# Token-major k, v and vs of the prompt: 32x32 block transposes and 128-byte transfers in the place of TensorE transposes

## The reference

```python
h = rms_norm(x, g_pre);  z = h @ w_in            # 1024 x 3072
q, k, v, ga, u, vs, gg = split(z)                # 512, 256, 256, 512, 512, 512, 512 columns
att  = attend(q, k, v)                           # block-sparse attention, prompt: own and past blocks of 256
u    = gelu(u);  v_rows = group_layer_norm(gelu(vs), g_sgu)      # 8 groups of 64 channels
gm   = u * (tril(w_s[g]) v_rows + b[g])          # inside chunks of 128 tokens
y    = x + rms_norm(concat(att * silu(ga), gm * silu(gg)) @ w_out, g_post)
return y, k, v, v_rows                           # k, v rows are outputs, v_rows for the sample alone
```

## Time and profile before

| | us |
|---|---|
| median of 3 runs | 288.61 |
| lowest, highest | 286.06, 288.98 |
| the profiled execution | 285.58 |
| its span, first to last instruction | 283.9 |

### The profile page before, as it was taken

The page is one execution under the profiler, slowest core; times in us unless marked ns, Lnnn a source line. Parts: engine busy times, 40 slices in busy tenths (PEclk is TensorE's granted clock), DMA queues, the critical chain, the costliest instruction groups (busy, mean ns, idle before and its releaser), DMA issues.

```text
span 283.9 us, 6071 instructions
## 1 busy us (share of the span) xinstructions
PE 272.5 (96%) x2140; PEld 237.2 (84%) x2140; DVE 196.0 (69%) x447; ACT 154.6 (54%) x353; POOL 69.7 (25%) x85
## 2 busy tenths in 40 slices
PE   8999999999999999999899999999899999999992
PEld 2789998998997887999687999998799976767881
DVE  1794886599935335826649889899979894927763
ACT  5974459541694323178886466555364563628611
POOL 4547003300311040333033452432450510000000
PEclk9999999999999999999999999999999999999998
DMA  7969993349998898831445018022007604040042
GB/s 244 330 179 223 286 244 90 135 153 274 245 315 247 260 300 216 267 112 41 149 135 172 2 37 224 1 67 84 0 2 271 193 1 148 2 149 2 18 187 109
DMA packets 37602, 43.39 MB, mean 153 GB/s; under 512 B 2963, under 2 KB 32659, under 8 KB 37572
## 3 DMA queue, kind: packets, MB, share of 16 engines
q1 hardware_dynamic: 36626, 40.25, 46.9%
q0 software_dynamic: 944, 2.75, 3.7%
q10 hardware_dynamic: 2, 0.00, 0.0%
HBM read 39.59 MB, written 3.41 MB: 151 GB/s over the span
## 4 chain that ended last, share of the span: by engine, by line
PE 75%; DVE 12%; ACT 8%; issue 3%; DVEq 0%; POOL 0%; ACTq 0%; POOLq 0%
PE Z L1386 12%; PE Z L1387 12%; PE Z L1388 12%; PE T L1307 4%; PE S L1425 3%; DVE probs L1205 3%; PE O L1524 2%; PE Z L1343 2%; PE O L1460 2%; PE S L1343 2%; PE Z L1345 2%; PE S L1344 2%; PE Z L1344 2%; PE S L1345 2%; DVE pT_lo L1211 2%
## 5 line engine op out<-in xcount | busy, mean ns | idle before, releaser
L1386 PE MATMUL Z<-act_hi,w_hi 128*128 128x256 f32 (+1 forms) x352 | 102.9, 292 | 0.6 <-ACT zvs L839 0.3
L1387 PE MATMUL Z<-act_lo,w_hi 128*128 128x256 f32 (+1 forms) x352 | 101.8, 289 | 0.0
L1388 PE MATMUL Z<-act_hi,w_lo 128*128 128x256 f32 (+1 forms) x352 | 101.5, 288 | 0.0
L1386 PEld LDWEIGHTS Z<-act_hi,w_hi 128*128 128x128 f32 x352 | 66.5, 189 | 2.9 <-issue 2.0
L1387 PEld LDWEIGHTS Z<-act_lo,w_hi 128*128 128x128 f32 x352 | 66.4, 189 | 0.0
L1388 PEld LDWEIGHTS Z<-act_hi,w_lo 128*128 128x128 f32 x352 | 66.3, 188 | 0.0
L678 POOL TENSOR_TENSOR w_lo<-w_raw,w_hi 128x1024 fp32r<-128x1024 f32 x16 | 38.2, 2389 | 67.0 <-ACT w_hi L764 67.0
L764 ACT ACTIVATE w_hi<-w_raw 128x1024 fp32r<-128x1024 f32 x32 | 33.5, 1051 | 15.0 <-DMA w_raw<-in_w_out 9.8
L980 DVE TENSOR_TENSOR w_lo<-w_raw,w_hi 128x1024 fp32r<-128x1024 f32 x16 | 19.3, 1211 | 16.0 <-ACT w_hi L764 16.0
L906 ACT ACTIVATE probs<-S,nmax 128x128 f32<-128x128 f32 (+3 forms) x32 | 16.6, 523 | 23.0 <-DVE nmax L1195 21.7
L1082 DVE STREAM_TRANSPOSE kT<-k_ring 128x1024 f32<-128x1024 f32 x16 | 19.7, 1238 | 0.6 <-PE S L1425 0.5
(11 more groups left out here) (253 smaller groups left out, 532.3 us busy)
## 6 DMA issues: line engine op xcount, KB each, us to landing
w_raw<-in_w_in SPq DMA_DIRECT2D x11, 1024.0 KB, 7.0
k_ring<-in_cache_k SPq DMA_DIRECT2D x64, 128.0 KB, 3.2
v_ring<-in_cache_v SPq DMA_DIRECT2D x64, 128.0 KB, 4.3
w_raw<-in_w_out SPq DMA_DIRECT2D x8, 512.0 KB, 4.3
x_sb<-in_x_prompt SPq DMA_DIRECT2D x4, 512.0 KB, 5.6
x_res<-in_x_prompt SPq DMA_DIRECT2D x4, 512.0 KB, 5.3
out<-y_sb SPq DMA_DIRECT2D x8, 256.0 KB, 2.0
w_raw<-in_w_in SPq DMA_DIRECT2D x2, 512.0 KB, 6.4
```

The lines of the kernel that those rows point to most:

```text
L1386: mm(out, wh[:, k, :], act_hi[:, k, cols], start=(k == 0), stop=False)
L1387: mm(out, wh[:, k, :], act_lo[:, k, cols], start=False, stop=False)
L1388: last = mm(out, wl[:, k, :], act_hi[:, k, cols], start=False, stop=(k == KD - 1))
```

## The change

For the four full token tiles the transposes on PE go. DVE turns each 128x512 tile of `kv32` (`KVB` 0 to 3: k0, k1, v0, v1) and of `zvs` (`VSB` 0 to 3) in place as 32x32 blocks. Each block then stands in the right orientation but in the wrong place, and transfers that POOL issues put it right: four for each tile, each of 32 partitions with 16 pieces of 128 bytes, 512 pieces. For k and v they go straight to the outputs; v is then read back as rows (`v_tok`, 512 KB), and one ACT and one DVE instruction of 128x1024 make `v_st` (`VST`). For vs they go to a DRAM tensor `vs_rows`, from which one transfer of 1 MB fills `vn`. The layer norm of those tiles (`VLN`) runs from `vn` in SBUF, tiles 0 and 1 behind halves 28 and 29 (behind round two's `DEX 1`), tiles 2 and 3 behind 31 and 32. `VSN 4` moves from half 31 to 24, `LN` from 32 to 33, `LNM` from 33, 35, 37, 39, 41 to 34, 36, 37, 39, 40.

New waits: POOL waits for the v transfers to land before the read back (in `KVB 3`, half 16), and for the vs transfers before the read of `vn` (in `VSB 3`, half 24); ACT waits at half 20 for `v_back`, DVE there for ACT; DVE waits at half 28 for `vs_moved`.

```diff
-    after(16, ("KVN", 4), ("KVN", 0))
-    for n, h in enumerate((17, 20, 22)):
-        after(h, ("KVN", 1 + n))
+    for j in range(4):
+        after(10 + 2 * j, ("KVB", j))
+    after(16, ("KVN", 4))
+    after(20, ("VST",))
...
-    for n, h in enumerate((24, 25, 28, 29)):
-        after(h, ("VSN", n))
+    for j in range(4):
+        after(18 + 2 * j, ("VSB", j))
+    after(24, ("VSN", 4))
+    for n, h in enumerate((28, 29)):
+        after(h, ("VLN", n))
...
-    after(31, ("VSN", 4))
-    after(32, ("LN",))
-    for n, tt in enumerate((4, 0, 1, 2, 3)):
-        after(33 + 2 * n, ("LNM", tt))
+    after(31, ("VLN", 2))
+    after(32, ("VLN", 3))
+    after(33, ("LN",))
+    for h, tt in zip((34, 36, 37, 39, 40), (4, 0, 1, 2, 3)):
+        after(h, ("LNM", tt))
... POOL
-                    pool.wait_ge(vst_done, 4)
-                    pool.wait_ge(stored_kv[1], 2 * 32)
+                    pool.wait_ge(vst_done, 1)
                     pool.dma_start(g_sgu_bc[:, :], ...)
+                elif kind == "KVB":
+                    j = s[1]
+                    out, landed = (k_prompt, stored_k) if j < 2 else (v_prompt, stored_v)
+                    rows = out[0, 0].rearrange("(b j) h d -> j b (h d)", j=32)
+                    pool.wait_ge(kv_turned, j + 1)
+                    for a in range(4):
+                        at = P * (j % 2) + 32 * a
+                        pool.dma_start(rows[:, :, at:at + 32], kv32[32 * a:32 * a + 32, j, 0:SEQ].rearrange("p (b i) -> p b i", i=32))\
+                            .then_inc(landed, 16)
+                    if j == 3:
+                        pool.wait_ge(stored_v, 8 * 16)
+                        pool.dma_start(v_tok[:, :, :], v_prompt[0, 0].rearrange("(t p) h d -> p t (h d)", p=P)).then_inc(v_back, 16)
+                elif kind == "VSB":
+                    j = s[1]
+                    rows = vs_rows.rearrange("(b j) c -> j b c", j=32)
+                    pool.wait_ge(vs_turned, j + 1)
+                    for a in range(4):
+                        at = P * j + 32 * a
+                        pool.dma_start(rows[:, :, at:at + 32], zvs[32 * a:32 * a + 32, j, 0:SEQ].rearrange("p (b i) -> p b i", i=32))\
+                            .then_inc(vs_out, 16)
+                    if j == 3:
+                        pool.wait_ge(kt_done, 16)
+                        pool.wait_ge(vs_out, 16 * 16)
+                        pool.dma_start(vn[:, 0:4, :], vs_rows.rearrange("(t p) c -> p t c", p=P)).then_inc(vs_moved, 16)
... ACT
+                elif kind == "VST":
+                    act.wait_ge(v_back, 16)
+                    nc.scalar.activation(v_st[:, :, :, 0:HD], v_tok[:, :, :].rearrange("p t (h d) -> p t h d", h=KVH), ACT.Copy).then_inc(vst_hi, 1)
+                elif kind == "VLN":
+                    act.wait_ge(centred, tt + 1)
+                    act.wait_ge(ssq_done, tt + 1)
+                    nc.scalar.activation(ln_sq[:, :], vn[:, tt, :], ACT.Square).then_inc(sq_done, 1)
... DVE
+                elif kind == "KVB":
+                    if j < 2:
+                        dve.wait_ge(k_first, 2 * j + 2)
+                    else:
+                        dve.wait_ge(z_free["act"], freed(Z_FREED_BY, HALF_AT[TILE_OF["v", j - 2], 1])[1])
+                    nc.vector.transpose(kv32[:, j, 0:SEQ], kv32[:, j, 0:SEQ]).then_inc(kv_turned, 1)
+                elif kind == "VST":
+                    dve.wait_ge(vst_hi, 1)
+                    nc.vector.tensor_tensor(v_st[:, :, :, HD:], v_tok..., v_st[:, :, :, 0:HD].bitcast(fp32), ALU.subtract).then_inc(vst_done, 1)
+                elif kind == "VSB":
+                    dve.wait_ge(z_free["act"], freed(Z_FREED_BY, HALF_AT[TILE_OF["vs", j], 1])[1])
+                    nc.vector.transpose(zvs[:, j, 0:SEQ], zvs[:, j, 0:SEQ]).then_inc(vs_turned, 1)
+                elif kind == "VLN":
+                    if tt == 0:
+                        dve.wait_ge(vs_moved, 16)
+                    link(nc.vector.tensor_reduce(ln_mu[:, 0, :], vt, AX.X, ALU.add))
+                    nc.vector.scalar_tensor_tensor(vt, ln_mu[:, 0, :]..., -1.0 / GCH, vt, ALU.mult, ALU.add).then_inc(centred, 1)
+                    dve.wait_ge(sq_done, tt + 2)
+                    nc.vector.tensor_reduce(ln_var[:, tt, :], ln_sq[:, :]..., AX.X, ALU.add).then_inc(ssq_done, 1)
```

More of the change, by code:

```diff
@@ L237, in build @@
     w_out_v = w_out[0].rearrange("(k p) c -> p k c", p=P)
+    vs_rows = nc.dram_tensor("vs_rows", [SEQ, 512], fp32).ap()
     def kv_rows(prompt, sample, tt):
@@ L291, in build @@
         R_V = region(4096 + 8192 + 10240)
-        kvn = place("kvn", [P, 2, 512], fp32, R_V)
+        v_tok = place("v_tok", [P, 4, KVW], fp32, R_V)
         ln_sq = place("ln_sq", [P, 512], fp32, R_V)
@@ L402, in build @@
         v_in = [sem(f"v_in{n}") for n in range(4)]
-        stored_kv = [sem("stored_kv0"), sem("stored_kv1")]
+        stored_k, stored_v, v_back = sem("stored_k"), sem("stored_v"), sem("v_back")
+        kv_turned, vs_turned, vs_out, vs_moved = (sem(n) for n in ("kv_turned", "vs_turned", "vs_out", "vs_moved"))
         stored_kvs = sem("stored_kvs")
@@ L636, in _ @@
             sp.wait_ge(stored_sgu, 16)
-            for n in range(2):
-                sp.wait_ge(stored_kv[n], 2 * 32)
+            sp.wait_ge(stored_k, 8 * 16)
+            sp.wait_ge(stored_v, 8 * 16)
             sp.wait_ge(stored_kvs, 32)
@@ L855, in _ @@
                     R = ROWS[tt]
-                    if 2 <= tt < 4:
-                        act.wait_ge(stored_kv[tt % 2], 32)
-                        act.wait_ge(vst_done, tt - 1)
-                    take(n, (kvn[:, tt % 2, :] if tt < 4 else kv_s[:, 0:512]), T[n % 2][0:R, :])
-                    if tt < 4:
-                        act.wait_ge(t_free["act"], freed(T_FREED_BY, n)[1])
-                        nc.scalar.activation(v_st[:, tt, :, 0:HD], kvn[:, tt % 2, KVW:].rearrange("p (h d) -> p h d", h=KVH), ACT.Copy)\
-                            .then_inc(vst_hi, 1)
+                    take(n, kv_s[:, 0:512], T[n % 2][0:R, :])
+                elif kind == "VST":
+                    act.wait_ge(v_back, 16)
+                    nc.scalar.activation(v_st[:, :, :, 0:HD], v_tok[:, :, :].rearrange("p t (h d) -> p t h d", h=KVH), ACT.Copy).then_inc(vst_hi, 1)
                 elif kind == "DEX":
@@ L1050, in _ @@
                             dve.wait_ge(t_full, T_OF["VSN", 4] + 1)
+                            dve.wait_ge(vs_moved, 16)
                         if what == "gg" and j == 0 and half == 0:
-                            dve.wait_ge(t_full, T_OF["KVN", 3] + 1)
+                            dve.wait_ge(t_full, T_OF["KVN", 4] + 1)
+                            dve.wait_ge(stored_k, 8 * 16)
+                            dve.wait_ge(stored_v, 8 * 16)
                         nc.vector.scalar_tensor_tensor(dst[:, j, cols], th[:, g % 2, 0:wide], 1.0, bank[:, 0:wide], ALU.add, ALU.mult)\
@@ L1070, in _ @@
                         .then_inc(t_free["dve"], 1)
[L1071 to L1076 removed]
+                elif kind == "KVB":
+                    j = s[1]
+                    if j < 2:
[5 more added lines that the diff above has]
+                    dve.wait_ge(vst_hi, 1)
+                    nc.vector.tensor_tensor(v_st[:, :, :, HD:], v_tok[:, :, :].rearrange("p t (h d) -> p t h d", h=KVH),
+                                            v_st[:, :, :, 0:HD].bitcast(fp32), ALU.subtract).then_inc(vst_done, 1)
+                elif kind == "VSB":
+                    j = s[1]
+                    dve.wait_ge(z_free["act"], freed(Z_FREED_BY, HALF_AT[TILE_OF["vs", j], 1])[1])
+                    nc.vector.transpose(zvs[:, j, 0:SEQ], zvs[:, j, 0:SEQ]).then_inc(vs_turned, 1)
+                elif kind == "VLN":
+                    tt = s[1]
+                    vt = vn[:, tt, :].rearrange("p (g c) -> p g c", g=GRP)
+                    if tt == 0:
+                        dve.wait_ge(vs_moved, 16)
+                    link(nc.vector.tensor_reduce(ln_mu[:, 0, :], vt, AX.X, ALU.add))
+                    nc.vector.scalar_tensor_tensor(vt, ln_mu[:, 0, :].unsqueeze(2).broadcast_to([P, GRP, GCH]), -1.0 / GCH, vt,
+                                                   ALU.mult, ALU.add).then_inc(centred, 1)
+                    dve.wait_ge(sq_done, tt + 2)
+                    nc.vector.tensor_reduce(ln_var[:, tt, :], ln_sq[:, :].rearrange("p (g c) -> p g c", g=GRP), AX.X, ALU.add).then_inc(ssq_done, 1)
                 elif kind == "KTR":
@@ L1514, in _ @@
                     if u == 0:
[L1515 removed]
+                        pe.wait_ge(vst_done, 1)
                         pe.wait_ge(own_taken, 1)
```

24 lines of the change are left out of this document (7 added, 17 removed).

## The result

The changed kernel takes 294.67 us in the median of six runs (290.88 to 295.91), the kernel before 286.34 beside it (285.9 to 288.98). The ratio is 1.016, 95% interval 1.009 to 1.023; run again later it was 1.015 (1.008 to 1.022). So the change is slower by 1.6% or more, where I had forecast 285.6 for a kernel before of 288.6, 1% faster, and had put 292.0 at the upper end of the range.

The account below looks back on a forecast made before the run. PE, busy 96% of the span, was taken as the bound, so work removed returns one for one. The terms -3.5 - 0.9 + 0.5 + 0.5 + 0.4 = -3.0 us gave a median of 285.6, range 283.5 to 292.

Parts of the forecast that it names:

- PE's savings: On PE: eight groups of four transposes gone, 3.5 us, and a wait for DVE at half 31 gone, 0.9 us.
- The wait on `vn`: PE's 0.9 us wait at half 31 loses its cause because `VSN 4` moves to half 24: -0.9 us.
- `KVB 0`: DVE's block transpose ahead of half 11's `k_lo` makes PE start half 13 later: 0.71 - 0.22 = +0.5 us.
- The pieces: Transfers in 128-byte pieces: 15 ns each, 15 us of all engines for 16,384, nearly fitting the spare DMA time.
- Rival A: Late transfers at 25 ns a piece stall PE 6 us at half 24 or 28: 291.6, at 50 ns 295; chance 0.26.
- The deadline on `v_ring`: Slot 5 lands at 103, PE reads it at 104, one us left: +0.5 us, bounds 0 to 6.
- `v_back`: Half 20: v read back by 90, ACT comes at 88.8 with nothing for PE until 94.86; covered by 5 us.
- The others: Deadlines `vs_out` for POOL's tile 14 low part, covered by 2.4 us, and `vs_moved` behind half 28, covered narrowly.
- Halves 28 to 34: DVE chain up to 2.75 us longer minus 1.06, PE 4 us earlier: +0.4 us for one bank wait, bounds 0 to 3.
- B: DVE and ACT chain of halves 28 to 34 sets the pace, all 2.75 us of `VLN 3` on PE: 288.0; chance 0.16.

Follow-up runs that it names:

- e13_again: Second run of the k and v part alone, POOL's low parts in four pieces, v slot 3 issued right behind slot 2, against the kernel before: ratio 0.986.
- e5: The changed kernel with POOL's low part of each slice cut into four instructions of 256 columns, against the kernel before: ratio 0.999.

## Why the prediction was wrong

- **PE's savings were right.** I had 3.5 + 0.9 = 4.4 us. Measured are 1.8 to half 22 and 3.0 from half 25 to 32, 4.8 us. The wait on `vn` is gone.
- **`KVB 0` was right**: +0.5 forecast, +0.41 found, and the wait for `k_lo` is on the list with 0.5. The block transpose took 0.67 to 0.69 us (0.71 estimated). That the stall went away with `KVB 0` behind half 11 and the kernel became 1.5 to 2% slower is a matter of the transfers, not foreseen and only in part explained.
- **The pieces were too dear.** I took 15 ns, with 25 and 50 as bounds; a piece costs its bytes, 6 ns, and at most some 3 more. Rival A's upper value, 295, is near the median of 294.67 for another reason, by luck. The Trainium skill, "DMA: Bandwidth & Descriptors", section Specifications, has a read-modify-write below 512 bytes; with it a piece would have cost the 50 ns of that value, and the traces do not agree.
- **The deadline on `v_ring`** was named as the weakest, and rightly, but for slot 5 and with +0.5. It was 3.0 and 0.7 us in two profiles, and part of it at slot 3, in half 23. The forecast took issue and usual landing, 4.3 us, and not how much slower a load can be in a full stretch: 7 to 8 us at most. Of the other deadlines, `v_back` had 5 us of cover in the sum and 0.3 in the profile: ACT waited 5.2 us for it, to 96.19, and half 21 ended at 96.50. That was hidden here; in e13_again it was 3.8 us late and was not. The others held: POOL's low part of tile 14 was done at 120.35, half 28 started at 124.41 with no wait.
- **Halves 28 to 34 failed: +0.4, and it was +8.4**, in halves 32 to 38. The step reasoned over the number and place of DVE's instructions, each at its old length, and that length was not theirs to keep. Two facts were at hand: the new centring has its input in SBUF instead of PSUM, and the LN multiplications move to other halves against POOL's low parts. Neither changes a duration by itself; both change what it overlaps with. A list of POOL's eleven instructions in 120 to 170 us beside the new places would have shown it. By e5, 5.1 of the 8.4 us are these holds and what follows from them, and 1.8 at most are the longer chain.
- On PE the 8.4 us are made up like this: gaps of 0.95, 0.79, 0.52, 0.30, 1.00 and 2.20 us are 5.8 (before has one of 0.4), and with the clock at 1.2 GHz behind the last one half 37 took 1.5 more. About 1 us I can't assign.

Of the rivals, B had the right place and the wrong mechanism (288.0); A had the right symptom for 1 to 3 us of it. None had an instruction that changes its length, and so the range ended too low.

## What to carry to other kernels

When a step moves on VectorE, or its input moves from PSUM to SBUF, lay the new place of each instruction that combines or scales SBUF tiles beside GpSimd's instructions that read SBUF. A hold lasts to the end of GpSimd's instruction, so try cutting those into pieces first (here 0.74 us and not 2.4): it gave 0.6% even to the tuned kernel, where a single long instance of an otherwise short instruction had given the stall away. A load with 1 us of cover in a stretch where the DMA engines are full is not covered; issue it earlier, in the place of one that waits for a buffer anyway. And look at when the queue issues it, not only at how long it takes to land.
